# One more feed-forward tile pair per layer by seven products, and the forget gate in four column groups

## What is computed

```python
# after each mixer, twice
h = ada_modulate(rms_norm(x, g_ffn[i]), sh2, sc2)
gate, up = split_cols(h @ w_in, (D_FF, D_FF))          # D_FF = 2816 = 22 tiles of 128
x = x + gt2[:, None, :] * ((jax.nn.silu(gate) * up) @ w_out)

# second mixer ("B"), forgetting attention
q, k, v, g, f = split_cols(h @ w_in, B_WIDTHS)         # f is 16 columns wide, one for each head
logf = jax.nn.log_sigmoid(f.astype(jnp.float32) + b_forget.astype(jnp.float32))
cum = jnp.cumsum(lf_all, axis=1)                       # over the keys, added to the attention logits
```

## Time and profile before

| | |
|---|---|
| median of 3 runs | 1533.57 us (1532.62 to 1533.8) |
| the profiled execution | 1533.63 us |
| its span in the trace | 1531.5 us |
| granted TensorE clock, mean | 0.992 of full speed |
| busy PE / DVE / ACT / POOL | 97% / 70% / 41% / 38% |

### The profile page before, as it was taken

How to read it: one execution, slowest core, us unless ns; L and a number is a source line. 1 busy time by engine, 2 the same in 40 slices (tenths; PEclk the granted TensorE clock), 3 DMA queues, 4 the chain that set the end, 5 groups by cost and what they waited for, 6 DMA issues and landing times.

```text
span 1531.5 us, 29136 instructions
## 1 busy us (share of the span) xinstructions
PE 1492.0 (97%) x11405; PEld 1373.2 (90%) x11405; DVE 1069.4 (70%) x2057; ACT 634.3 (41%) x1265; POOL 580.4 (38%) x346
## 2 busy tenths in 40 slices
PE   5999999999999999999999999999999999999998
PEld 2768956899999999999888888887999999999998
DVE  1659888668887778876644444457988877688753
ACT  3434366344552145522533333334254541355423
POOL 1234841225771066722322222231227640376421
PEclk8999999999999999999999999999999999999999
DMA  9874510341344433452254444443532355333521
GB/s 335 269 264 150 141 39 2 96 114 40 104 128 159 148 83 89 116 173 67 77 167 127 127 127 127 127 128 100 171 91 56 93 168 167 86 108 83 156 79 62
DMA packets 244454, 189.21 MB, mean 124 GB/s; under 512 B 12888, under 2 KB 228608, under 8 KB 240112
## 3 DMA queue, kind: packets, MB, share of 16 engines
...
## 4 chain that ended last, share of the span: by engine, by line
PE 86%; DVE 7%; ACT 3%; issue 2%; DMA 1%; POOL 0%; ACTq 0%; SPq 0%; POOLq 0%; DVEq 0%
PE lin L860 40%; PE lin L1440 28%; PE lin L877 5%; PE S L1201 2%; PE O L995 1%; PE O L1331 1%; PE O L1254 1%; DVE acc_out L2666 1%; PE T L1234 1%; PE S L1064 1%; DMA ada_raw<-in_w_ada 1%; PE S L1120 1%; ACT act_hi L1665 1%; PE lin L1300 1%; PE T L1291 0%
## 5 line engine op out<-in xcount | busy, mean ns | idle before, releaser
L2147 POOL TENSOR_TENSOR w_lo<-w_raw,w_hi 128x1024 fp32r<-128x1024 f32 (+3 forms) x68 | 168.3, 2476 | 409.6 <-ACT w_hi L1612 409.6
L2238 POOL TENSOR_TENSOR w_lo<-ada_raw,w_hi 128x512 fp32r<-128x512 f32 x114 | 156.9, 1378 | 241.8 <-ACT w_hi L1913 241.8
L1612 ACT ACTIVATE w_hi<-w_raw 128x1024 fp32r<-128x1024 f32 (+2 forms) x110 | 125.2, 1139 | 224.7 <-PE lin L860 212.3
L860 PE MATMUL lin<-act_hi,w_hi 128*128 128x288 f32 (+1 forms) x1088 | 164.6, 302 | 5.3 <-ACT act_hi L1644 2.0
L860 PE MATMUL lin<-act_hi,w_lo 128*128 128x288 f32 (+1 forms) x1088 | 167.3, 299 | 0.2
L860 PEld LDWEIGHTS lin<-act_hi,w_hi 128*128 128x128 f32 (+1 forms) x1088 | 149.5, 189 | 15.5 <-issue 10.1
L860 PE MATMUL lin<-act_lo,w_hi 128*128 128x288 f32 (+1 forms) x1088 | 162.1, 298 | 0.0
L860 PEld LDWEIGHTS lin<-act_hi,w_lo 128*128 128x128 f32 (+1 forms) x1088 | 149.9, 188 | 7.5 <-issue 6.7
L860 PEld LDWEIGHTS lin<-act_lo,w_hi 128*128 128x128 f32 (+1 forms) x1088 | 149.6, 188 | 3.4 <-issue 2.9
L2238 POOL TENSOR_TENSOR w_lo<-s_tmp,w_hi 128x512 fp32r<-128x512 f32 x76 | 129.2, 1717 | 15.0 <-ACT w_hi L1916 15.0
L1440 PE MATMUL lin<-act_hi,w_hi 128*128 128x288 f32 x608 | 105.4, 295 | 0.0
...
## 6 DMA issues: line engine op xcount, KB each, us to landing
...
```

The source lines that it names most:

```text
L860: last = nc.tensor.matmul(lin_u(u)[0:m, tok], w, (lo if p == 2 else hi)[:, at(t) if at else t, tok], start=(p == 0 and t == 0), stop=(p == ...
L1612: A(w_hi[:, u % 2, 0:n], w_raw[:, u % 2, 0:n], ACT.Copy).then_inc(whi_done, 1)
L2147: TT(w_lo[:, u % 2, 0:n], w_raw[:, u % 2, 0:n], w_hi[:, u % 2, 0:n].bitcast(F32), ALU.subtract)\
L2238: TT(ring(w_lo, q), raw, ring(w_hi, q).bitcast(F32), ALU.subtract).then_inc(ws_lo_p, 1)
```

## The change

`FULL` becomes 2: each layer makes 2 tiles directly and 20 by pairs, 9 in the first half and 11 in the second. The low parts of the units `u0 + 2` and `u0 + 3` and of `T` 0 and 1 go from GpSimd to VectorE, and VectorE's and ScalarE's start of a layer is reordered: `t_part` 2, the sum S4 and `T_lo` 2 now come after `full_gate(1)`, the last direct one.

The forget gate's unit goes. In its place TensorE makes, in the last third of `first_units`, plain float32 products of 32 weight columns (16 and 16 zeros) in four column groups of the array, k-tile `4r + j` in group `j`, on `fo` (the normed activations before the shift), and the same on the shift's two columns; `fold_w` adds the four groups when the result is turned. The running sums are made block by block and VectorE carries the last column on; they move behind unit `U_B + 2`. GpSimd waits for the end of the log-sigmoid chain before the low part of `U_B + 3`. The first turn of `b_body` is written out, with two thirds of its first unit ahead of the transposes.

```diff
-FULL = 3
+FULL = 2
-OUT_UNITS = [u0 + m for u0 in (U_OA, U_OB, *U_OUT) for m in range(1, KT)]
+OUT_UNITS = [U_F0 + 2, U_F0 + 3, U_B + 2, U_F1 + 2, U_F1 + 3] + [u0 + m for u0 in (U_OA, U_OB, *U_OUT) for m in range(1, KT)]
...
-            at += n in ((2, 3, 5, 6), (2, 4, 6))[h % 2]
+            at += n in ((3, 6), (2, 4, 6))[h % 2]
...
@@ tensor
+            def forget_gate():
+
+                pe.wait_ge(wf_in, 16)
+                pe.wait_ge(y_done, y_base(2, 1) + KT)
+                for r in range(2):
+                    for h in range(2):
+                        for j in range(4):
+                            kt = 4 * r + j
+                            nc.tensor.matmul(S[32 * j:32 * j + 32, h, 0:HALF], wf[:, kt, :],
+                                             fo[:, kt, h * HALF:(h + 1) * HALF], start=(r == 0), stop=(r == 1))
...
-            first_units(U_FG, 16, 2, ACT_N2)
-            pe.wait_ge(lin_free[U_FG % 2], free_count(U_FG))
+            first_units(U_B, P, 2, ACT_N2, forget_gate)
+            pe.wait_ge(z_done, 1)
...
-                    last = nc.tensor.matmul(S[0:16, 0, b * P:NP_], lf_tok[:, b, :], sums_w[:, 0:NP_ - b * P],
-                                            start=(b == 0), stop=(b == 3))
+                    last = nc.tensor.matmul(S[0:16, 0, b * P:(b + 1) * P], lf_tok[:, b, :], sums_w[:, 0:P],
+                                            start=True, stop=True)
...
+                        ahead = first and r == 0 and k == 0
+                        if ahead:
+                            lin_part(u, 0, KT, P, act_hi, act_lo)
+                            lin_part(u, 1, KT, P, act_hi, act_lo)
...
@@ scalar, ffn_stage
-                for j in (0, 2, 1):
-                    t_hi(layer, j)
-                in_tile(u0, base, 1, lambda: split_hi(u0 + 4, N))
-                split_hi(u0 + 5, N)
+                t_hi(layer, 0)
+                t_hi(layer, 1)
 
                 def first_parts():
                     hi_part(n0, W_S1)
                     hi_part(n0, W_A11)
-
-                in_tile(u0, base, 2, first_parts)
-                hi_part(n0, W_S2)
+                    hi_part(n0, W_S2)
+
+                in_tile(u0, base, 1, first_parts)
                 hi_part(n0, W_S3)
+                t_hi(layer, 2)
...
@@ gpsimd
+            split_lo(U_B + 1, N)
+            pool.wait_ge(lf_dve, LF_DONE)
+            split_lo(U_B + 3, N)
...
@@ vector, ffn_stage
                 t_part(layer, nz, 0)
                 full_gate(0, NB)
-                t_part(layer, nz, 2)
+                split_lo(u0 + 2, KT * P)
+                t_part(layer, nz, 1)
                 full_lo(0)
-                t_part(layer, nz, 1)
+                t_lo(layer, 0)
+                split_lo(u0 + 3, KT * P)
                 t_part(layer, nz, 3)
-                t_lo(layer, 2)
-                full_gate(1)
-                full_lo(1)
+                t_lo(layer, 1)
                 if layer == 1:
                     sum_mods(5)
                 first_sums(n0)
-                full_gate(2)
-                full_lo(2)
+                full_gate(1)
+                t_part(layer, nz, 2)
+                s_add(n0, W_S4)
+                t_lo(layer, 2)
+                full_lo(1)
                 pair_stage(n0, n0 + N_A)
```

More of the change, by code:

```diff
@@ L61 @@
 U_F0 = U_OA + KT
-FULL = 3
+FULL = 2
 U_F0B = U_F0 + 2 * FULL + KT
-U_FG = U_F0B + KT
-U_B = U_FG + 1
+U_B = U_F0B + KT
 U_OB = U_B + 4 * PAIRS
@@ L797, in _ @@
             w_load(U_B + 4, wb[:, P:2 * P], KT, P)
+            w_load(U_B + 5, wb[:, D + P:D + 2 * P], KT, P)
             sp.wait_ge(lf_dve, LF_CUM)
@@ L807, in _ @@
             mid_load(1, 1)
-            for c in range(1, 4):
+            for c in range(2, 4):
                 w_load(U_B + 4 + c, wb[:, c * D + P:c * D + 2 * P], KT, P)
@@ L961, in first_units @@
                     half_part(u + 1, 1, KT, P, act_hi, act_lo, [(0, kt)])
+                if late is not None:
+                    late()
                 for p in (1, 2):
@@ L1463, in _ @@
             ffn_stage(0, 1, ACT_N1, {2: 0}, {0: 1, 5: 2})
-            first_units(U_FG, 16, 2, ACT_N2)
-            pe.wait_ge(lin_free[U_FG % 2], free_count(U_FG))
+            def forget_gate():
[7 more added lines that the diff above has]
+                                             fo[:, kt, h * HALF:(h + 1) * HALF], start=(r == 0), stop=(r == 1))
+                for r in range(2):
+                    for j in range(4):
+                        kt = 4 * r + j
+                        last = nc.tensor.matmul(S[32 * j:32 * j + 32, 0, HALF:HALF + 2], wf[:, kt, :],
+                                                mods[:, SHIFT[2] + kt, :], start=(r == 0), stop=(r == 1))
+                last.then_inc(fg_done, 1)
+            first_units(U_B, P, 2, ACT_N2, forget_gate)
+            pe.wait_ge(z_done, 1)
             t_use(T_LF)
+            zf = zb[:, :, :].rearrange("p a c -> p (a c)")
             for t in range(5):
                 c = t * P if t < 4 else TOK - P
-                last = nc.tensor.transpose(T[:, t * 16:(t + 1) * 16], zb[:, c:c + P], ident[0:16, 0:16])
+                last = nc.tensor.matmul(T[:, t * 16:(t + 1) * 16], zf[:, c:c + P], fold_w[:, 0:16], start=True, stop=True)
             last.then_inc(t_ready, 1)
@@ L1577, in b_body @@
                         pv_unit(k, n, PAIRS + r, t + 1, it, 8, 26, pT_b, pTs_b, vS_b[:, r, :, :], True)
-                        for half in range(2 if nxt else 0):
+                        for half in range(2 if nxt and not ahead else 0):
                             if k == 2:
@@ L2238, in lo_part @@
                 TT(ring(w_lo, q), raw, ring(w_hi, q).bitcast(F32), ALU.subtract).then_inc(ws_lo_p, 1)
-            def t_lo(layer, j):
-                pool.wait_ge(th_done, 4 * layer + (1 if j == 0 else 3))
-                pool.wait_ge(t_raw, 4 * layer + (3 if j == 0 else 4))
-                TT(T_lo[:, j, :, :], T_raw[:, j, :, :], T_hi[:, j, :, :].bitcast(F32), ALU.subtract)\
-                    .then_inc(tl_p, 1)
             def pair_stage(n0, n1, u_out):
-                for i in (W_A11, W_S2, W_S3):
+                for i in (W_S2, W_S3):
                     lo_part(n0, i)
@@ L2261, in ffn_stage @@
                 u0, n0 = U_IN[layer], layer * N_ALL
-                for u in range(u0 + 1, u0 + 2 * FULL):
-                    split_lo(u, N)
-                for j in range(2):
-                    t_lo(layer, j)
+                split_lo(u0 + 1, N)
+                lo_part(n0, W_A11)
                 pair_stage(n0, n0 + N_A, U_OUT[2 * layer])
                 out_stage(U_OUT[2 * layer], 0)
+                lo_part(n0 + N_A, W_A11)
                 pair_stage(n0 + N_A, n0 + N_ALL, U_OUT[2 * layer + 1])
@@ L2932, in _ @@
             chain(V.scalar_tensor_tensor(sums_w[:, 0:P], tri, NEG, ident, ALU.is_equal, ALU.add))
+            split_lo(U_B + 2, KT * P)
             dve.wait_ge(t_ready, T_LF + 1)
@@ L2949, in _, with carry_on @@
             dve.wait_ge(cum_done, 1)
-            chain(V.tensor_scalar(cum[:, 0:NP_], S[0:16, 0, 0:NP_], -1.0 / QSCALE, None, ALU.mult))
+            def carry_on(bank, c0, c1, at):
+                before = cum[:, at + c0 - 1:at + c0].broadcast_to([16, c1 - c0])
+                chain(V.scalar_tensor_tensor(cum[:, at + c0:at + c1], S[0:16, bank, c0:c1], -1.0 / QSCALE, before,
+                                             ALU.mult, ALU.add))
+            chain(V.tensor_scalar(cum[:, 0:P], S[0:16, 0, 0:P], -1.0 / QSCALE, None, ALU.mult))
+            for c in range(1, 4):
+                carry_on(0, c * P, (c + 1) * P, 0)
             dve.wait_ge(cum_done, 2)
-            chain(V.tensor_scalar(cum[:, NP_:], S[0:16, 1, 0:PAST + NS], -1.0 / QSCALE, None, ALU.mult))
+            chain(V.tensor_scalar(cum[:, NP_:NP_ + P], S[0:16, 1, 0:P], -1.0 / QSCALE, None, ALU.mult))
+            carry_on(1, P, 2 * P, NP_)
+            carry_on(1, PAST, PAST + NS, NP_)
             assert steps[0] == LF_CUM
```

112 lines of the change are left out of this document (60 added, 52 removed).

## The result

| | before | after |
|---|---|---|
| median us (runs) | 1533.2 (8) | 1537.13 (8) |
| lowest to highest | 1531.42 to 1534.16 | 1536.12 to 1537.93 |
| profiled execution: span | 1531.5 | 1534.3 |

The change made the kernel slower: ratio 1.0027, 95% interval 1.0018 to 1.0036, some 4 us. The profiled execution is the fastest of the eight, 1536.12 us, and the least typical in its clock: its mean granted clock is 0.993 of full speed, that of the other seven 0.989 to 0.991. The forecast was 1532.1, no change to speak of, with 1526.5 to 1538.0 as its range: the time lies in the range, on the side that had a chance of 0.25.

What follows compares the result with a forecast made beforehand. The prediction took TensorE, with 86% of the chain, to bound the kernel. Its terms, -3.2 - 0.4 + 8.8 - 6.7 = -1.5 us against the profiled 1533.63, gave 1532.1 us, range 1526.5 to 1538.

Steps and rivals of the forecast that it cites:

- the place of the tiles: Tiles allocated behind the new bias_z: the forecast had no term for their shift, so matmuls on hid stood at no change.
- the clock: TensorE's clock behind the new waits: the sum gave a fall no cost and left it to the second rival.
- -3.2 and -0.4, the matmuls saved: Direct units: 12 matmuls less per layer, -3.2 us; less waiting for GpSimd's low part, -0.4 us.
- +8.8, the start of the pairs: First pair of each layer: TensorE waits for late VectorE and ScalarE results, 4.4 us a layer, +8.8 us in both.
- my first rival: Start of the pairs: GpSimd seldom gets between VectorE's instructions, 0.5 to 2 us a layer, time 1525.7; chance 0.2.
- -6.7, the gate: Forget gate: unit gone -6.4, shorter running sums -1.9, waits gone -1.0, new float32 matmuls +2.6; together -6.7 us.
- The thin cover: Before mixer B's first softmax transposes: softmax done about 775, TensorE there at 775.2; bk 2 us later would cost 2.
- the second rival: Start of the pairs: the new waits let the clock fall; 1535.5 us with one fall, 1538.9 with one per layer; chance 0.22.
- the third rival: Ahead of layer 1: the present fall of the clock goes away, time 1528.7 us; chance 0.08.
- the column groups: Forget gate's float32 matmuls: forecast to overlap, +2.6 us; rival, no overlap or bk late, +4 to +6, 1537; chance 0.08.

Runs made afterwards that it cites:

- b2: b1 with one GpSimd wait more: the low part of S3 in each layer's first pair waits for VectorE's third T_raw; 1531.21 us, ratio 0.9988.
- a4: Kernel before with only the forget gate's part of the change, no tile moved, three full tile pairs per layer; 1527.04 us, ratio 0.9959.
- c3: a4 without the 36 matmuls of the next linear ahead of the first transposes in mixer B's attention; 1532.81 us, ratio 1.0000.
- a1: Changed kernel, both parts, with bias_z inside bias_f's tile so that no later tile moves 32 bytes; 1534.85 us, ratio 1.0009.
- a2: Kernel before with an unused 32-byte tile where the change puts bias_z, so every later tile moves; 1534.17 us, ratio 1.0005.
- b3: a4 with an unused 32-byte tile ahead of the weights, moving them and everything behind; 1526.03 us, ratio 0.9958.
- b4: b3 with a second unused 32-byte tile at bias_z's place, so hid and what follows stand 64 bytes later; 1528.1 us, ratio 0.9968.
- a3: Kernel before with only the feed-forward part (FULL = 2, low parts on VectorE, new order), gate and tiles as before; 1538.28 us, ratio 1.0035.
- b1: a1 with VectorE's hid_lo of the second full pair and next block's first sum put behind the first Z; 1531.47 us, ratio 0.9989.
- c1: b2 with VectorE's second combination right behind the first, then the low part of the fourth T, and hid_lo earlier; 1530.72 us, ratio 0.9985.
- c2: c1 with an unused 32 bytes ahead of the weights; 1528.55 us, ratio 0.9965.
- c4: a4 without the wait that holds GpSimd's low part until VectorE has the gate's logarithms; 1527.48 us, ratio 0.9969.

## Why the prediction was wrong

The sum was -3.2 - 0.4 + 8.8 - 6.7 = -1.5 us; +3.9 was measured, and the direction was wrong. Two terms that the sum put at nothing failed, the place of the tiles and the clock, and two were mis-sized. Term by term:

- **-3.2 and -0.4, the matmuls saved.** Right as work: 852 matmuls against 864 in layer 0, from the second direct tile to the first block on `hid`. Of the old stall only GpSimd's share went, as said.
- **+8.8, the start of the pairs.** The mechanism was right and the size too small. Forecast per layer: 1.6 before S3, 0.3 and 0.2 behind it, 2.2 before S4, 0.7 before A22. Measured: 1.75, small ones, 2.03, 0.36; the stage came out 3.1 us longer in layer 0, where the clock did not fall, and 4.4 - 1.6 - 0.2 = 2.6 was forecast: 0.5 us short in each layer. `t_part` 2 took 4.49 us as the turns of GpSimd had it. The Trainium skill, "SBUF — State Buffer", "SBUF: two separate sides", calls the shared pair of ports an exclusive lock held for a whole instruction; b2 agrees, at 1.04 us given back for one GpSimd instruction taken away, and VectorE did not keep the pair between its instructions, as my first rival needed.
- **-6.7, the gate.** -5.9 by a4's median, about -5 by the traces, so 0.8 to 1.7 us too much was expected. The stretch to the first transposes, with the 36 matmuls taken out, is 6.3 us shorter, near the forecast; what the ledger left out is that about 0.9 us were given back in the next unit, where TensorE waits 0.73 us for `pT_b` in a row that had no such wait. The thin cover was real: in c3 the softmax is ready at 775.03, and the forecast had it at 775. That the cover just held in the changed kernel is partly luck, since the margin forecast was 0.2 us.
- **Nothing, the place of the tiles: the 32 bytes.** The largest step that failed. The matmuls on `hid` stood in the sum at no change. They took 2.1 us more; the two stages on `hid` are 2.0 us longer in the trace, and a1 without the shift is 2.3 us faster in the median. The diff showed the new tile; I read it as two columns, not as a shift of everything behind it. Of all the terms this one is shown best, by a1, a2, b3 and b4.
- **Nothing, the clock.** The other step that failed. The waits were costed as time alone; the fall behind them was left to the second rival at 0.22. In the four kernels with 1.7 us or more before S3 (after, a1, a3, b1) it came at seven of eight starts of the pairs, for 3.4 us each time, which is 1.7 us of full speed lost; in the three with 0.8 us or less there (b2, c1, c2) at none of six. The Trainium skill, "TensorE: Matmul & The Clock Gate", "What's actually happening", lets the clock follow how busy the engine has been lately; the runs agree. But neither 1.7 us nor the rival's 3.4 is what a fall adds to the time. One between the two waits added nothing to be seen (+3.0 for the stage in a3's layer 0, +3.1 without a fall), since it shortened the wait behind it (0.86 in place of 2.03). One behind the wait for Z made it +4.0 and +4.3, so about 1 us more.

By the stages of the changed kernel's trace: the pairs 3.1 + 4.3 = 7.4 us where 5.2 was forecast, 1.2 of the difference by the late fall in layer 1 and 1.0 by the size of the waits; `hid` 2.0 where nothing was; the gate about -5 where -6.7 was. That is -1.5 + 2.2 + 2.0 + 1.7 = +4.4, where +3.9 was measured with an interval from 2.8 to 5.5. The closeness is in part luck, because the two profiled executions are not alike in their clocks. The kernel before has its long fall ahead of layer 1, which is missing after; this was the third rival, at 0.08, and it is worth 1.5 to 1.9 us and not the 3.4 of the forecast. Against it, the other runs of the changed kernel had more falls than the profiled one: their mean granted clock over all eight is 0.9902, with a1 at 0.9904 and a3 at 0.9910, and the kernel before had 0.9923 to 0.9930 in three sets of 21 or 22 runs. That is 3 to 4 us of full speed more lost in an execution, so the kernels with the long waits lose more clock in their runs too, and not only in one trace; where in those runs the falls came is not recorded.

The parts measured alone, 5.3 and -5.9, and the shift give +1.5, and a1 is 2.5 us above a3 and a4 together. Within the intervals (up to 2 us to either side each) this can be chance. By the stages a1 is 1.0 us above, all of it in layer 0's pairs, where it waits 2.0 us for Z and a3 0.9. I leave open what the rest is.

Of the other rivals, the fall ahead of layer 1 goes and comes between executions and kernels (missing in after, a2, b2, c3 and c4, there in the others), which no change here decides, and eight of the kernels' traces (a3, b1 to b4, c1, c2 and c4) have a like one ahead of layer 0, which the kernel before does not; and the column groups did overlap, 2.4 us for 2.6 forecast.
